# A delta rule's inverse on one Trainium2 core: its 128-row products made as two 64 by 64 products on the diagonal

## The reference, cut to what matters

```python
def gdn_block(S, q, k, v, g, beta):
    ...
    strict = jnp.tril(jnp.ones((L, L), dtype=bool), -1)
    ...
    a_mat = jnp.where(strict, bt[..., :, None] * kk * dec, 0.0) + jnp.eye(L, dtype=jnp.float32)
    ...
    sol = lax.linalg.triangular_solve(a_mat, rhs, left_side=True, lower=True)
    u = sol[..., :A_DV] - jnp.einsum('bhjd,bhdv->bhjv', sol[..., A_DV:], S)
    ...
```

## Time and profile before

| | before |
|---|---|
| median of 3 runs | 3380.09 us |
| lowest and highest | 3379.20 and 3380.52 us |
| the profiled execution's span | 3380.3 us |
| TensorE matmuls, busy | 3315.0 us (98%) |
| VectorE busy | 1493.2 us (44%) |
| ScalarE busy | 1120.0 us (33%) |
| GpSimd busy | 504.3 us (15%) |
| granted TensorE clock | nine tenths or more of full speed in every slice |

### The profile page before, as it was taken

The page is one execution under the profiler, slowest core; times in us unless marked ns, Lnnn a source line. Parts: engine busy times, 40 slices in busy tenths (PEclk is TensorE's granted clock), DMA queues, the critical chain, the costliest instruction groups (busy, mean ns, idle before and its releaser), DMA issues. The chain is left out here.

```text
span 3380.3 us, 47319 instructions
## 1 busy us (share of the span) xinstructions
PE 3315.0 (98%) x16389; PEld 2602.6 (77%) x16389; DVE 1493.2 (44%) x3534; ACT 1120.0 (33%) x2854; POOL 504.3 (15%) x506
## 2 busy tenths in 40 slices
PE   8999999999899999999999999899999999999999
PEld 5777777777588888888777666788888888777676
DVE  3555555665355555555443224233442334343233
ACT  4344334343234444444310243133332333210341
POOL 1453454453200000000001001000000000011000
PEclk9999999999999999999999999999999999999999
DMA  5211132112331212212452102111111111461101
GB/s 157 61 41 34 31 27 33 33 33 89 91 63 48 46 34 37 49 48 54 140 187 75 38 1 64 51 40 43 55 43 54 40 40 54 143 211 56 38 1 52
DMA packets 245828, 205.95 MB, mean 61 GB/s; under 512 B 20143, under 2 KB 222799, under 8 KB 245671
## 3 DMA queue, kind: packets, MB, share of 16 engines
q1 hardware_dynamic: 240318, 194.29, 22.2%
q10 hardware_dynamic: 5360, 9.67, 0.7%
HBM read 157.95 MB, written 45.99 MB: 60 GB/s over the span
## 5 line engine op out<-in xcount | busy, mean ns | idle before, releaser
L510 PE MATMUL gdn_pj<-hT,Wb 128*128 128x352 f32 x1536 | 518.1, 463 | 4.9 <-ACT gdn_zraw L747 3.4
L510 PEld LDWEIGHTS gdn_pj<-hT,Wb 128*128 128x128 f32 x1536 | 267.1, 193 | 95.0 <-issue 5.2
L2071 PE MATMUL gla_pj<-gla_TX,gla_S 128*128 128x256 f32 (+1 forms) x736 | 191.2, 393 | 0.0
L2071 PE MATMUL gla_pj<-hT,gla_S 128*128 128x256 f32 (+1 forms) x736 | 187.1, 393 | 0.0
L1762 ACT ACTIVATE band_E<-band_NS,band_nm 128x576 f32<-128x576 f32 (+9 forms) x136 | 89.8, 660 | 212.7 <-DVE band_nm L1892 212.2
L2071 PEld LDWEIGHTS gla_pj<-hT,gla_S 128*128 128x128 f32 x736 | 139.4, 190 | 26.2
L2071 PEld LDWEIGHTS gla_pj<-gla_TX,gla_S 128*128 128x128 f32 x736 | 138.2, 190 | 26.2
L1216 POOL TENSOR_TENSOR x_kept<-gdn_AT,gdn_level 128x384 f32<-128x384 f32 x144 | 144.3, 1034 | 35.7 <-DVE gdn_TT L998 18.5
L2071 PE MATMUL band_pj<-hT,band_S 128*128 128x288 f32 (+1 forms) x512 | 142.4, 395 | 0.0
L2071 PE MATMUL band_pj<-band_TX,band_S 128*128 128x288 f32 (+1 forms) x512 | 140.6, 395 | 0.0
L2071 PE MATMUL band_pj<-hT,Wb 128*128 128x256 f32 x512 | 136.2, 387 | 3.5 <-PEq L45 2.1
(11 more groups left out here) (530 smaller groups left out, 6670.1 us busy)
## 6 DMA issues: line engine op xcount, KB each, us to landing
Wb<-in_l_w_in_dram SPq DMA_DIRECT2D x95, 512.0 KB, 7.1
fin_xT<-x_features SPq DMA_DIRECT2D x16, 528.0 KB, 7.5
fin_R<-o_features SPq DMA_DIRECT2D x16, 528.0 KB, 10.1
Wb<-in_l_w_mkv_dram SPq DMA_DIRECT2D x8, 1024.0 KB, 5.5
Wb<-in_l_w_out_dram SPq DMA_DIRECT2D x16, 512.0 KB, 4.2
o_features<-gla_OF ACTq DMA_DIRECT2D x14, 528.0 KB, 7.6
gla_Wv<-in_l_w_in_dram SPq DMA_DIRECT2D x7, 1024.0 KB, 5.3
gdn_GB<-gate_rows SPq DMA_DIRECT2D x8, 544.0 KB, 3.6
```

The costliest lines, as they stand in the source:

```text
L510: mm = pe.matmul(pj[:, m % 2, 0:w], W[:, j, k, :], hT[:, k, c0:c0 + w], start=k == 0, stop=k == KD - 1)
L2071: mm = pe.matmul(bank[:, 0:w], left(name, k), right(name, k, unit[0], w), start=name in ("P1", "P5", "P2") and k == 0, stop=k == FAST_K - ...
```

## The change

Four edits, all in `gdn`:

- TensorE: each product of the V and the X block becomes two, one for each 64 by 64 block on the diagonal: rows 0 to 63 with columns 0 to 63, and rows 64 to 127 with columns 64 to 127. Weights, moving data and output are the quarters of the same tiles; both outputs of a product go to the same PSUM bank, on different partitions.
- ScalarE: the copy of a group becomes two, each of 64 partitions and 3 times 64 columns.
- VectorE: the subtraction of a group likewise. The transpose stays whole.
- TensorE's loop over heads 1 to 6 becomes straight code; the other engines keep theirs.

```diff
+        HALVES = (slice(0, 64), slice(64, 128))
...
                             for t in range(3):
-                                mm = pe.matmul(P3[:, g, 128 * t:128 * t + 128], BT[:, 3 * g + t, :], TM[:, 3 * g + t, :],
-                                               start=True, stop=True)
+                                for P in HALVES:
+                                    c = 128 * t + P.start
+                                    mm = pe.matmul(P3[P, g, c:c + 64], BT[P, 3 * g + t, P], TM[P, 3 * g + t, P], start=True, stop=True)
                             mm.then_inc(v_done, 1)
...
                             for t in range(3):
-                                mm = pe.matmul(X3[:, g, 128 * t:128 * t + 128], VV[:, 3 * g + t, :], TT[:, 3 * g + t, :],
-                                               start=True, stop=True)
+                                for P in HALVES:
+                                    c = 128 * t + P.start
+                                    mm = pe.matmul(X3[P, g, c:c + 64], VV[P, 3 * g + t, P], TT[P, 3 * g + t, P], start=True, stop=True)
                             mm.then_inc(x_done, 1)
...
-                with pe.Fori(1, H_A - 1) as h:
+                for h in range(1, H_A - 1):
                     head(h, True, True)
...
-                            act.activation(g3(VV, g), p3(P3, g), ACT.Copy).then_inc(v_out, 1)
+                            for P in HALVES:
+                                mm = act.activation(g3(VV, g)[P, :, P], p3(P3, g)[P, :, P], ACT.Copy)
+                            mm.then_inc(v_out, 1)
...
-                            dve.tensor_tensor(g3(TT, g), g3(TT, g), p3(X3, g), ALU.subtract).then_inc(tt_ok, 1)
+                            for P in HALVES:
+                                mm = dve.tensor_tensor(g3(TT, g)[P, :, P], g3(TT, g)[P, :, P], p3(X3, g)[P, :, P], ALU.subtract)
+                            mm.then_inc(tt_ok, 1)
```

## The result

The changed kernel takes **3403.76 us** (median of 3 runs, 3403.37 to 3404.16) where the kernel before takes 3380.09: a ratio of 1.0069, 95% interval 1.0055 to 1.0083. It is 23.7 us slower, above the range of the prediction (3347 to 3392); the forecast was 16.5 us faster. The profiled execution spans 3402.1 us, 21.7 more than the one before. The granted clock is the same within 0.001 (0.992 and 0.993).

A forecast was written before the change was run, and what follows sets the result against it. TensorE's queue bounds the kernel, then VectorE's loop at 5.55 us a level against 5.79: 2.15 us a head, 15 in seven heads, 1.4 in the last, 16.5 off the median gives 3363.6 us; range 3347 to 3392.

The forecast's parts named there:

- Part 4: ScalarE and VectorE: halved subtraction costs 0.08 us more a group (bounds 0 and 0.15); ScalarE's longer copies are covered by TensorE's step.
- What bounds the kernel, and what is late next: Levels: TensorE's queue, 5.79 us a level, bounds; VectorE's loop, about 5.5, is next, GpSimd's 5.32 the third.
- Part 1: TensorE's loop over heads: writing it out gains at most 0.6 us in total, taken as nothing.
- Part 2: V and X blocks: 64 by 64 halves run side by side, 0.031 us a pair, 1.1 us a block.
- rivals without overlap: V and X blocks: halves run one after another; with switches paid 3414.5 us (chance 0.19), without switches 3386.5 (0.10).
- the one bound by issuing: V and X blocks: halves overlap but issue only every 0.038 us, 1.72 a block; 3372.5 us, chance 0.08.
- Part 3: Tile-size changes around each V and X block: 0.15 us in, 0.20 out, 0.35 a block, so a block costs 1.45.
- rival of free switches: V and X blocks: tile-size changes cost nothing for 64-row tiles, GpSimd's 5.3 ends last; 3351 us, chance 0.10.
- the head's gain of 2.15: One head: 0.45 us up to the first X block, 1.0 over four loops, 0.7 at the last X block.
- the first term: Each head up to the start of the first X block: 0.45 us gained.
- the slower side: V and X blocks: halves don't overlap but switches are paid, 2.44 us a block; 34 us slower, 3414.5, chance 0.19.
- The last paragraph's third condition: Prediction is wrong if the same gaps show elsewhere in a head: before the first V block or behind the levels.

The follow-up runs named there:

- the packed layout: Changed kernel with both quarters of a tile in the same 64 columns, on partitions 0-63 and 64-127, so nothing is split: 3338.33 us, ratio 0.9875 to the kernel before.

## Why the prediction was wrong

The step that failed is the subtraction of Part 4: it was put at 0.08 us a group more, and it is 0.27. Forecast and measurement are 40 us apart, 38 in the traces. Of these, 18 lie in the seven heads apart from VectorE's branches (15 gained forecast, 3.0 lost measured), and the subtraction is 16 of them (0.57 us in 4 levels of 7 heads). The late start is 9.2 and VectorE's branches are 7.5, which the prediction had no term for; the last head with the step to the next mixer is 5.3 (1.4 gained forecast, 3.9 lost measured, of which 3.0 for loads), and 1.9 came back behind it.

**What bounds the kernel, and what is late next:** right, and it decided. The loop through VectorE was 0.3 us from TensorE's own; it was the cover, and it was what the change used up.

**Part 1, the loop over heads costs nothing:** right for the loop by itself (3377.88, ratio 0.9994). What it left out is that the loop's code and the small products together make TensorE's program a third longer, and the program with 8595 rows starts 8 to 10 us later, whatever the added rows are. Nothing in the trace of before shows this. It is the largest part of the 21.7 us against the kernel before, and the second of the distance to the forecast.

**Part 2, pairs of 64 by 64:** right. The halves run side by side in one PSUM bank. The 36 of an X block take 1.26 us with the last one's 0.22, so they start 1.04/35 = 0.030 us apart, where 0.031 was forecast. The rivals without overlap and the one bound by issuing are out. So is, here, the rule of the Trainium skill ("TensorEngine Tiling (Array Packing)", Gotcha 1) that different row tiles cannot use one PSUM bank at the same time, for tiles that write to different output partitions: here the measurement decides.

**Part 3, switches of 0.35 a block:** right within a few hundredths. In the raw trace the last step ahead of the V block starts at 561.931; it holds the array for 0.295, and the first small load starts at 562.318, 0.09 late. Behind an X block the last small matmul starts at 560.790, the next full one at 560.939, and the one after it 0.40 later instead of 0.295: 0.25 in all, where 0.20 stood. The rival of free switches is out.

**Part 4, the subtraction: the term that failed.** It was put at 0.08 us a group, between 0 and 0.15; it is 1.36 - 1.09 = 0.27. I had the duration of one nearly right (0.34 forecast, 0.345 and 0.358 measured). The error was the overlap. The 0.07 taken off was that of a transpose with the whole subtraction behind it, and the halves have none: the second starts 0.36 behind the first and the transpose 0.39 behind that, 0.75 where the forecast comes to 0.66. And the overlap that was there is lost: the next group's first half starts when the transpose has ended, 0.61 behind its start instead of 0.51. In the packed layout, with single subtractions on 128 partitions, it is back: the next one starts 0.08 before the transpose ends (524.27 against 524.35). Three groups too small by 0.19 are 0.57 us a level, and 5.55 + 0.57 = 6.12 where 6.09 was measured. With whole subtractions the same sum gives 5.55 - 0.24 = 5.31, and 5.32 was measured. So the rest of the sum held, and this one term turned 0.25 gained a level into 0.30 lost. With it the head's gain of 2.15 becomes 0.45 - 4 x 0.30 + 0.7, nothing; measured were 0.3 lost. The rest is in the first term: from the first V block to the first X block it is 2.52 us in head 4 where it was 2.77, so 0.25 gained and not 0.45.

**What was missing: VectorE's own loop.** The change adds 15 instructions to VectorE's body. I had costed their time and not their number. Bodies of 289 to 295 rows in the trace branch back in 0.3 us, those of 304 in 3.4, five times, and 1.5 us of each reaches TensorE: 7.5 us, shown by taking the branch away and by lengthening the body of the kernel before.

**The rivals:** the slower side was held for possible through the products themselves (3414.5); the time came out between, for none of the rivals' reasons. The last paragraph's third condition, gaps elsewhere in a head, came nearest.

What stays open: why the transfers of the first 25 us, and the loads in front of the next mixer, move more slowly with some programs; whether it is the length or the place of VectorE's body that decides, since both changed together; why 4 to 5 of the 7.5 us that writing out VectorE's loop should have brought are missing from the total; and whether the halves don't overlap because they use 64 partitions or because neighbours begin at different ones (0 and 64). Not tried: letting ScalarE make the first projection's copies ahead of its wait for the three small loads. By the waits above this should shorten TensorE's 12.9 us.

## What to carry to other kernels

When one engine's work is cut in halves, ask what the cut does to every engine that reads the result: one instruction on 128 partitions became two on 64 that each cost nearly as much (0.35 us for 192 columns on 64 partitions, 0.32 to 0.35 for 192 columns on 128), and here they don't overlap. A layout that puts both halves side by side on the partitions keeps one instruction and makes it shorter; that was worth 65 us over the split one, of which 7.5 are the branches. And count instructions as well as time: of each engine that loops, how long its body gets, and how long the whole program gets, and look for the price at the backward branch and in the first loads.

## What the runs showed of the hardware

- Small products of different rows and different output partitions start 0.007 us apart in the same PSUM bank; 36 matmuls of 64 by 64 by 64 in 32 bits take 1.26 us.
- A subtraction of 192 columns on 64 partitions takes 0.35 us, one of 192 columns on 128 partitions 0.32 to 0.35 and one of 384 columns 0.52 to 0.56: here the columns count and the partitions don't. The one on 128 partitions starts 0.08 us before the transpose ahead of it ends; the one on 64 starts 0.03 after.
- A backward branch of VectorE's costs 0.3 us with a body of 289 to 295 rows in the trace and 3.4 to 3.6 with 304, along with five more 8 KB instruction packets each time.
- Loads that no edit touched can take longer in another program: 82 to 100 GB/s in the five microseconds from 15 to 20, in every one of seven traces of programs with 8595 TensorE rows, and 39 with 9096, where five traces of shorter programs show 180 to 262. This repeats from execution to execution.
